# Layer 0 of a hybrid diffusion backbone: the linear recurrence's steps placed between the projections' units

## The chip, the cores and the metric

One core of one Trainium2 chip. The metric is device time in microseconds (us) of one execution of the whole program, the median of several runs. A profiled execution of the kernel before gives the spans, the busy times and the waits that are read here; "the profile" and "the trace" mean that execution.

## The reference, cut to what matters

Two layers over 512 sample tokens and 128 prompt tokens (640 in all), width 1024. The change touches layer 0 alone, the even one:

```python
def even_mixer(h, l, P, rope, ctx):
    z = jnp.dot(h, P['w_in_ab'][li])
    xa, ga, qd, kd, vd = split_last(z, (LRU_WIDTH, LRU_WIDTH, DIFF_QK, DIFF_QK, DIFF_V))   # 512 columns each
    y_a, lru_state = rglru_mixer(xa, ga, ...)
    q = rms_norm(qd), k = rms_norm(kd), v = vd       # per head; then rope on q and k of the sample
    o = diff_attention(q, k, v)
    y = concatenate([y_a, rms_norm(o) * (1 - lam_init)])
    return jnp.dot(y, P['w_out'][l])

def rglru_mixer(xa, ga, ...):
    u = centred_depthwise_conv(xa, conv_w) + conv_b             # 4 taps along the tokens
    # for each of two directions:
    r = sigmoid(u @ w_a + b_a);  i = sigmoid(u @ w_i + b_i)     # block-diagonal 64 x 64
    a = exp(-8 * r * softplus(-lam));  b = sqrt(1 - a**2) * (i * u)
    h = linear_recurrence(a, b, h0)                             # h[t] = a[t] h[t-1] + b[t]
    y = (h_f + h_b) * gelu(ga)
```

The modulation of both layers (shift, scale and gate, `silu(c) @ w_mod + b_mod`) does not depend on the tokens. The kernel computes it in 24 chunks of 512 columns, in the gaps that its order leaves.

## The kernel before, in words

All data is fp32. TensorE (PE), VectorE (DVE), ScalarE (ACT), GpSimd (POOL) and the DMA queue of SyncE (SP) each run an instruction order written out by hand; semaphores tie them together. Everything that PE produces goes to one of four PSUM pairs (two banks each), handed out in strict rotation (`take`, L168): the n-th unit of work gets pair n mod 4 and waits until the unit four places earlier was released by the engine that reads it (`release`, L183).

Layer 0's input projection is five chunks of 512 columns (2 MB of weights each). Chunks 0 (xa) and 1 (ga) are computed channel-major in four units each (`proj_T_pe`, L670: f = 0 to 3), chunks 2, 3, 4 (q, k, v) token-major in three units each (`proj_R_pe`, L689: two token tiles, two, one). ACT and DVE copy the units out in turns (`read_T` L712, `read_R` L722).

A modulation chunk i has four stages: PE multiplies (`mod_rows_pe`, L450), ACT copies the sums out (`mod_act`, L475), PE transposes them (`mod_turn_pe`, L466), DVE adds them up (`mod_dve`, L528). Chunks 4 to 7 stand between the five projections, chunks 8 to 13 inside the recurrence, chunks 14 to 19 inside the attention.

The recurrence (`lru_pe` L766, `lru_act` L783, `lru_dve` L823) comes after the last projection. It has eight steps i = 2 ct + d (four channel tiles, two directions). In a step PE computes two gate units (L773, L774), ACT does Tanh, Tanh, Exp, Tanh (L794 to L800) and later Sqrt (L805), and DVE does three elementwise operations (the "input", L831 to L834), then a multiply and two scans (L842 to L847) and, for d = 1, two adds and the product with gelu(ga) into `hT` (L853 to L857). Two sets of buffers (`lb`) alternate, so ACT's step i waits for DVE's scans of step i-2 (L793). ACT runs gates(i), then root(i-1); DVE runs input(i), then scan(i-1).

While the projections run, DVE does the convolution (L815) and, for q and then k, `diff_rows_dve` (L998): normalization over five tiles and rope, with ACT's Square and Sqrt in front (`diff_rows_act`, L939). After the recurrence `diff_pe` (L1065) transposes k and q, issues three filler matmuls (`keep_busy`, L1084) and starts the 20 steps of the attention with `scores` (L1089).

SP issues all weight loads in one order (`load_stream`, L1499). A chunk goes to one of three ring slots; before its load SP waits until PE has read the slot's previous chunk (`read_by_now`, L1495), and everything behind it in the order waits too. Before, slot = position mod 3:

```python
s = i % 3 if l == 0 or i < 6 else i % 2
```

Of the kernel before, what the change touches and what calls it, by code (L numbers as in the profile page):

```python
# [78 lines left out]
def build(nc, io, outs):  # L79
    with ExitStack() as ctx:  # L80
# [139 lines left out]
        def mmk(pe, out, lhs, rhs):  # L220

            for k in range(KD):
# [17 lines left out]
        for l in range(2):  # L240
            for i, c in enumerate(chunks[l]):
                s = i % 3 if l == 0 or i < 6 else i % 2
                slot_uses[s] += 1
                slot_of[c] = (s, slot_uses[s])
                loads.append((c, s, last_in_slot.get(s)))
                last_in_slot[s] = c
            base = list(slot_uses)
            for s in range(6):
                slot_uses[s] += NE // 2
                slot_of["exp", l, s] = base[s]  # L250
            loads.append((("experts", l), None, dict(last_in_slot)))
            for s in range(3):
                last_in_slot[s] = ("experts", l)
# [416 lines left out]
        def proj_T_pe(pe, l, c):  # L670

            w = arrived(pe, ("in", l, c, 0))
            for f in range(4):
                u = ("pT", l, c, f)
                ps = take(pe, u)
                lhs = lambda k: w[:, k, f * P:f * P + P]
                if l == 0 and c == 0 and f == 0:

                    for k in range(KD):
                        h_here(pe, l, 0, k)  # L680
                        pe.matmul(ps[:, 0:NS], lhs(k), hT[:, k, 0:NS], start=(k == 0), stop=(k == KD - 1))
                        last = pe.matmul(ps[:, NS:T], lhs(k), hT[:, k, NS:T], start=(k == 0), stop=(k == KD - 1))
                    finish(last, u)
                    continue
                mmk(pe, ps[:, 0:NS], lhs, lambda k: hT[:, k, 0:NS])
                finish(mmk(pe, ps[:, NS:T], lhs, lambda k: hT[:, k, NS:T]), u)
            chunk_last["in", l, c, 0] = u

        def proj_R_pe(pe, l, c):  # L689

            w = arrived(pe, ("in", l, c, 0))
            n = chunk_src(("in", l, c, 0))[1]
            for tp in range(3):
                u = ("pR", l, c, tp)
                ps = take(pe, u)
                if l == 1 and c == 4 and tp == 0:

                    keep_busy(pe, ps, 2)
                    for k in range(KD):
                        h_here(pe, l, 0, k)  # L700
                        for t in range(2):
                            last = pe.matmul(ps[:, 512 * t:512 * t + n], hT[:, k, t * P:t * P + P], w[:, k, 0:n],  # L702
                                             start=(k == 0), stop=(k == KD - 1))
                    finish(last, u)
                    continue
                for t in range(2 * tp, min(2 * tp + 2, NT)):
                    o = 512 * (t % 2)
                    last = mmk(pe, ps[:, o:o + n], lambda k: hT[:, k, t * P:t * P + P], lambda k: w[:, k, 0:n])
                finish(last, u)
            chunk_last["in", l, c, 0] = u  # L710

        def read_T(eng, l, c, dst, part, padded):  # L712
            for f in range(part, 4, 2):
                u = ("pT", l, c, f)
                ps = filled(eng, u)
                if padded:
                    copy(eng, dst[:, f, PS0:PS0 + NS], ps[:, 0:NS]).then_inc(S("pad_evac" + str(part)), 1)
                    release(copy(eng, dst[:, f, PP0:PP0 + NP], ps[:, NS:T]), u)
                else:
                    release(copy(eng, dst[:, f, :], ps[:, 0:T]), u)  # L720

        def read_R(eng, l, c, dst, part):  # L722
            n = chunk_src(("in", l, c, 0))[1]
            if l == 0 and c == 2:
                eng.wait_ge(S("y_room0"), 16)
                eng.wait_ge(S("y_room1"), 16)
            for tp in range(3):
                if (tp + c) % 2 == part:
                    u = ("pR", l, c, tp)
                    ps = filled(eng, u)  # L730
                    m = 2 if tp < 2 else 1
                    release(copy(eng, dst[:, 2 * tp:2 * tp + m, :],
                                 ps.rearrange("p (a b) -> p a b", a=2)[:, 0:m, 0:n]), u)
# [9 lines left out]
        lb = [[hflat[:, 2560 + 0 * UW:2560 + UW], hflat[:, 2560 + UW:2560 + 2 * UW],  # L743
               hflat[:, 2560 + 2 * UW:2560 + 3 * UW], ar(7716, UW)],
# [21 lines left out]
        def lru_pe(pe):  # L766
            pe.wait_ge(S("late_here"), LATE_ALL)
            for ct in range(4):
                pe.wait_ge(S("u_ready"), ct + 1)
                for q in range(4):  # L770
                    u = ("gate", ct, q)
                    ps = take(pe, u)
                    pe.matmul(ps[:, 0:NS], wg[:, q, ct, :], uT[:, ct, 0:NS], start=True, stop=True)  # L773
                    finish(pe.matmul(ps[:, NS:UW], wg[:, q, ct, :], uT[:, ct, NS:UW], start=True, stop=True), u)  # L774
                    if q % 2 == 1:

                        i = 2 * ct + q // 2
                        if i < N_LRU_MODS:
                            mod_rows_pe(pe, 8 + i)
                        if i <= N_LRU_MODS:  # L780
                            mod_turn_pe(pe, 7 + i)

        def lru_act(act, step):  # L783
            act.wait_ge(S("qk_rows"), 1)
            for i in range(9):
                if i < 8:
                    ct, d = i // 2, i % 2
                    tr, ti, a, _ = lb[i % 2]
                    c8 = 4 * d + ct
                    if i == 0:  # L790
                        filled(act, ("pR", 0, 4, 2))
                    if i >= 2:
                        act.wait_ge(S("lru_scan"), i - 1)  # L793
                    release(act.activation(tr, filled(act, ("gate", ct, 2 * d))[:, 0:UW], ACT.Tanh, scale=0.5,  # L794
                                           bias=hba[:, c8:c8 + 1]), ("gate", ct, 2 * d))
                    release(act.activation(ti, filled(act, ("gate", ct, 2 * d + 1))[:, 0:UW], ACT.Tanh, scale=0.5,
                                           bias=hbi[:, c8:c8 + 1]), ("gate", ct, 2 * d + 1))
                    emptied(act, ("gate", ct, 2 * d))
                    step(act.activation(a, tr, ACT.Exp, scale=hs[:, c8:c8 + 1], bias=hs[:, c8:c8 + 1]))
                    act.activation(tr, tr, ACT.Tanh, scale=hs[:, c8:c8 + 1], bias=hs[:, c8:c8 + 1])\  # L800
                        .then_inc(S("lru_tanh"), 1)
                if i >= 1:
                    act.wait_ge(S("lru_q"), i)
                    tr = lb[(i - 1) % 2][0]
                    act.activation(tr, tr, ACT.Sqrt, scale=-0.25).then_inc(S("lru_root"), 1)  # L805
                if i < N_LRU_MODS:
                    mod_act(act, 8 + i)
# [7 lines left out]
        def lru_conv_dve(v, step):  # L815
            for part in range(2):
                v.wait_ge(S("pad_evac" + str(part)), 2)
            for ct in range(4):
                emptied(v, ("pT", 0, 0, ct))
                conv_dve(v, step, uT[:, ct, :], xap[:, ct, :], lambda tap: cB[:, lw_col + 4 * tap + ct:lw_col + 4 * tap + ct + 1],  # L820
                         cB[:, cb_col + ct:cb_col + ct + 1]).then_inc(S("u_ready"), 1)

        def lru_dve(v, step):  # L823
            filled(v, ("pR", 0, 4, 2))
            v.wait_ge(S("u_ready"), 4)
            for i in range(9):
                if i < 8:

                    tr, ti, a, w = lb[i % 2]
                    v.wait_ge(S("lru_tanh"), i + 1)  # L830
                    step(v.tensor_tensor(w, a, a, ALU.mult))  # L831
                    v.scalar_tensor_tensor(out=tr, in0=w, scalar=1.0, in1=tr, op0=ALU.add, op1=ALU.mult)\
                        .then_inc(S("lru_q"), 1)
                    step(v.scalar_tensor_tensor(out=ti, in0=ti, scalar=1.0, in1=uT[:, i // 2, :], op0=ALU.add,  # L834
                                                op1=ALU.mult))
                if i >= 1:
                    j = i - 1
# [1977 lines left out]
```

## Time and profile before

| what | us |
|---|---|
| median of 3 runs | 1795.73 (1794.01 to 1798.09) |
| the profiled execution's own time | 1794.16 |
| its span, first to last instruction | 1791.7 |
| PE busy in the span | 1607.9 (90%) |
| DVE / ACT / POOL busy | 633.5 / 439.5 / 239.3 |
| mean granted TensorE clock | 0.953 |

A row of the windows view gives a stretch, its length, then busy us (and instructions) of PE, PE's weight loads, DVE, ACT and POOL, the granted TensorE clock (1.00 is 2.4 GHz, 0.50 is 1.2 GHz), the share of the DMA engines and GB/s. A timeline row gives start, duration, engine, line and operation, and in brackets the idle time before it and what ended it; neighbouring instructions overlap by some hundredths, so the text takes differences of starts where it can.

Times in the text are positions in the span of 1791.7 us. The 2.5 us between the span and the execution's time lie outside what the trace shows and are taken as unchanged; the median of the three runs stands 1.57 us above the profiled execution.

### The profile page before, as it was taken

The numbers are of one execution on the slowest core, as the hardware profiler recorded it, in microseconds if no ns is written. First come the engines' busy times: TensorE is split into PE (matmuls) and PEld (weight loads), VectorE is DVE, ScalarE is ACT, GpSimd is POOL, SyncE is SP. The second block draws the span as 40 slices with busy tenths as digits, with TensorE's granted clock in tenths as the row PEclk, the third lists the DMA queues.
The fourth block names the chain that finished last, engine by engine and source line by source line (L and its number), as shares of the span: only waits on it lengthen the run. The fifth ranks groups of instructions, "written<-read, shape, count | busy, mean of one in ns | idle before, by whom it ended". The sixth has DMA issues, their size and how long they took to land.

```text
span 1791.7 us, 37993 instructions
## 1 busy us (share of the span) xinstructions
PE 1607.9 (90%) x16758; PEld 1040.3 (58%) x16758; DVE 633.5 (35%) x1290; ACT 439.5 (25%) x734; POOL 239.3 (13%) x237
## 2 busy tenths in 40 slices
PE   5999976999959999999999989888899959999992
PEld 2554434664527677676555558666675536776761
DVE  4234466652260000003129646645462270000003
ACT  3211175551031111102110246432231031111110
POOL 0000000000001111100000026156440000111113
PEclk8999997999969999998999999999899979999996
DMA  9932281244218999994121100011115227999994
GB/s 341 307 115 94 100 288 46 95 142 188 94 74 307 385 382 394 380 379 143 47 71 71 50 1 1 1 50 50 49 50 200 73 85 247 372 388 387 386 394 142
DMA packets 90319, 330.09 MB, mean 184 GB/s; under 512 B 10708, under 2 KB 16456, under 8 KB 82024
## 3 DMA queue, kind: packets, MB, share of 16 engines
q1 hardware_dynamic: 76016, 287.29, 42.1%
q0 software_dynamic: 9168, 32.65, 6.6%
q10 hardware_dynamic: 5032, 8.65, 1.3%
q8 instruction: 80, 1.31, 0.3%
q14 instruction: 23, 0.19, 0.0%
HBM read 303.79 MB, written 24.78 MB: 183 GB/s over the span
## 4 chain that ended last, share of the span: by engine, by line
PE 83%; DVE 9%; ACT 3%; issue 2%; DMA 2%; POOL 0%; ACTq 0%; DVEq 0%
PE pairs L223 27%; PE pairs L1396 16%; PE pairs L1408 12%; PE pairs L1379 2%; PE pairs L343 2%; PE pairs L1096 2%; PE pairs L1110 1%; PE pairs L1886 1%; PE pairs L1866 1%; PE pairs L2093 1%; PE pairs L1849 1%; PE pairs L490 1%; PE pairs L461 1%; PE pairs L2104 1%; PE pairs L702 1%
## 5 line engine op out<-in xcount | busy, mean ns | idle before, releaser
L223 PE MATMUL pairs<-hT,ring 128*128 128x128 f32 (+1 forms) x1120 | 306.2, 436 | 2.2 <-ACT hT L357 2.2
L223 PEld LDWEIGHTS pairs<-hT,ring 128*128 128x128 f32 x1120 | 170.3, 192 | 139.0 <-issue 139.0
L357 ACT ACTIVATE arena<-pairs 128x512 f32<-128x512 f32 (+6 forms) x212 | 123.7, 602 | 430.3 <-PE pairs L223 198.8
L223 PE MATMUL pairs<-ring,hT 128*128 128x512 f32 (+1 forms) x448 | 177.4, 557 | 0.0
L1396 PEld LDWEIGHTS pairs<-arena,ring 128*64 128x64 f32 x4096 | 142.9, 137 | 13.6 <-issue 13.6
L1396 PEld LDWEIGHTS pairs<-arena 128*64 128x64 f32 x4096 | 142.8, 137 | 13.2 <-issue 13.1
L1396 PE MATMUL pairs<-arena 128*64 128x80 f32 x4096 | 145.5, 233 | 1.6 <-ACT arena L1431 1.0
L1396 PE MATMUL pairs<-arena,ring 128*64 128x80 f32 x4096 | 145.8, 233 | 0.5 <-issue 0.5
L223 PEld LDWEIGHTS pairs<-ring,hT 128*128 128x128 f32 x448 | 84.8, 190 | 92.1 <-issue 89.1
L1464 DVE TENSOR_SCALAR hT<-pairs,arena 80x512 f32<-80x512 f32 x32 | 23.9, 747 | 272.0 <-ACT hT L1440 272.0
L1408 PE MATMUL pairs<-ring,arena 128*80 128x512 f32 x256 | 112.7, 593 | 0.2 <-DMA ring<-in_exp_w 0.2
L1408 PE MATMUL pairs<-arena 128*80 128x512 f32 x256 | 112.5, 592 | 0.0
L1460 DVE TENSOR_TENSOR arena<-hT,pairs 128x160 f32<-128x160 f32 x64 | 20.5, 321 | 249.3 <-PE pairs L1396 249.3
L357 DVE COPY arena<-pairs 128x512 f32<-128x512 f32 (+7 forms) x37 | 25.2, 703 | 185.1 <-PE pairs L223 178.7
L1491 POOL DMA_INDIRECT moe_rows<-hT,arena x32 | 45.4, 1420 | 293.7 <-DVE hT L1464 293.7
L1408 PEld LDWEIGHTS pairs<-ring,arena 128*80 128x80 f32 x256 | 37.7, 152 | 63.1 <-issue 62.9
L1408 PEld LDWEIGHTS pairs<-arena 128*80 128x80 f32 x256 | 37.8, 153 | 62.6 <-issue 62.6
L1440 ACT ACTIVATE hT<-pairs,arena 80x512 f32<-80x512 f32 x32 | 21.9, 683 | 212.1 <-PE pairs L1408 212.1
L1431 ACT ACTIVATE arena<-pairs 128x640 f32<-128x640 f32 x32 | 22.5, 703 | 185.6 <-PE pairs L1379 185.6
L1189 DVE SCALAR_TENSOR_TENSOR xT<-pairs,modt,xT 128x512 f32<-128x512 f32 x24 | 18.0, 750 | 140.8 <-PE pairs L223 125.7
L343 PE MATMUL pairs<-cst 128*128 128x512 f32 x118 | 63.4, 680 | 3.8 <-ACT arena L357 2.1
L1481 POOL DMA_INDIRECT hT<-h_rows,arena x32 | 29.4, 917 | 241.3 <-PE pairs L1379 199.5
(393 smaller groups left out, 2139.6 us busy)
## 6 DMA issues: line engine op xcount, KB each, us to landing
arena<-in_exp_w SPq DMA_DIRECT2D x48, 2048.0 KB, 18.8
ring<-in_exp_w SPq DMA_DIRECT2D x48, 2048.0 KB, 20.1
ring<-in_w_mod SPq DMA_DIRECT2D x24, 2048.0 KB, 8.2
ring<-in_w_in_ab SPq DMA_DIRECT2D x5, 2048.0 KB, 11.9
ring<-in_w_in_cd SPq DMA_DIRECT2D x5, 2048.0 KB, 7.8
ring<-in_w_out SPq DMA_DIRECT2D x4, 2048.0 KB, 8.8
moe_rows<-arena POOLq DMA_DIRECT2D x2, 2560.0 KB, 12.8
h_rows<-arena POOLq DMA_DIRECT2D x2, 2560.0 KB, 8.2
```

Source lines behind the costliest of these rows:

```text
L223: last = pe.matmul(out, lhs(k), rhs(k), start=(k == 0), stop=(k == KD - 1))
L343: pe.matmul(ps[:, 0:512], ident, cst[:, 0:4, :].rearrange("p a b -> p (a b)"), start=True, stop=True)
L357: return eng.activation(dst, src, ACT.Copy) if eng is nc.scalar else eng.tensor_copy(dst, src)
L1096: pe.matmul(ps[:, 0:512], q, k[:, 0:512], start=True, stop=True)
L1379: last = pe.transpose(ps[:, o:o + CAP], xe[par][:, k::KD], ident[0:CAP, 0:CAP])
L1396: last = pe.matmul(lin_of(j, f)[c:c + 64, :], w[:, k, f * P + c:f * P + c + 64], rhs, start=(k == 0), stop=(k == KD - 1))
L1408: last = pe.matmul(PSUM[0:CAP, 3, 512 * half:512 * half + 512], hid[par][:, f, :], w2[:, f, 512 * half:512 * half + 512], start=(f == 0), ...
L1431: act.activation(xeT[par], ps, ACT.Copy).then_inc(pair_free[0], 1)
L1440: act.activation(ye[par][:, 0:512], PSUM[0:CAP, 3, 0:512], ACT.Copy, scale=gateT[:, bass.ds(i, 1)])\
L1464: v.tensor_scalar(ye[par][:, 512:1024], PSUM[0:CAP, 3, 512:1024], gateT[:, bass.ds(i, 1)], None, ALU.mult).then_inc(pair_free[3], 1)
L1481: g.indirect_dma_start(xe[e % 2], None, DR["h", l], off(e)).then_inc(S(f"gathered{e % 2}"), 16)
L1491: g.indirect_dma_start(DR["m", l], off(e), ye[e % 2], None, compute_op=ALU.add)\
```

## The change

1. The order of loads and their slots are given by a list. From modulation chunk 4 to chunk 13, ten chunks, all go through slot 2, one after the other; the projections' chunks alternate between slots 1 and 0.
2. The projections are cut into single units (`proj_T_one`, `proj_R_one`, `read_T_one`, `read_R_one`), and the recurrence into `gates_pe`, `lru_gates_act`, `lru_root_act`, `lru_conv_dve(ct)`, `lru_input_dve(i)`, `lru_scan_dve(j)`. Three new functions, `layer0_pe`, `layer0_act` and `layer0_dve`, write out one order each, with a pair of gate units behind projection units from (1, 0) to (3, 0) and modulation chunks 4 to 13 between them.
3. `diff_rows` of q and of k come after the recurrence on ACT and DVE. The product with gelu(ga) is done for all four channel tiles after the last scan, into a tile `yT` of its own; ACT copies it to `hT` in steps 4 to 7 of the attention, and the output projection waits for these copies.
4. `lb`'s first set and rope's scratch move to other places of the arena; the sum of the two directions goes back into `uT`.

The diff, cut to its core:

```diff
-        N_LRU_MODS = 6
-        chunks = [all_mods[:4] + [c for p in zip(ins[0], all_mods[4:8]) for c in p] + ins[0][4:] + all_mods[8:20] +
-                  wouts[0], ins[1] + all_mods[20:] + wouts[1]]
+        chunks = [all_mods[:4] + ins[0][0:1] + all_mods[4:5] + ins[0][1:2] + all_mods[5:6] + ins[0][2:3] +
+                  all_mods[6:8] + ins[0][3:4] + all_mods[8:11] + ins[0][4:5] + all_mods[11:20] + wouts[0],
+                  ins[1] + all_mods[20:] + wouts[1]]
+        first_slots = [0, 1, 2, 0, 1, 2, 0, 2, 1, 2, 2, 0, 2, 2, 2, 1, 2, 2, 2, 0, 2, 1, 0, 2, 1, 0, 2]
...
-                s = i % 3 if l == 0 or i < 6 else i % 2
+                s = first_slots[i] if l == 0 else i % 3 if i < 6 else i % 2
...
+        yT = ar(9480, 4, T)
+        lb = [[ar(i * UW, UW) for i in range(4)],
...
+        def gates_pe(pe, i):
+            ct = i // 2
+            if i == 0:
+                pe.wait_ge(S("late_here"), LATE_ALL)
+            pe.wait_ge(S("u_ready"), ct + 1)
+            for q in (2 * (i % 2), 2 * (i % 2) + 1):
+                u = ("gate", ct, q)
+                ps = take(pe, u)
+                pe.matmul(ps[:, 0:NS], wg[:, q, ct, :], uT[:, ct, 0:NS], start=True, stop=True)
+                finish(pe.matmul(ps[:, NS:UW], wg[:, q, ct, :], uT[:, ct, NS:UW], start=True, stop=True), u)
...
+        def layer0_pe(pe):
+            for f in range(4):
+                proj_T_one(pe, 0, 0, f)
+            mod_rows_pe(pe, 4)
+            proj_T_one(pe, 0, 1, 0)
+            mod_turn_pe(pe, 4)
+            gates_pe(pe, 0)
+            proj_T_one(pe, 0, 1, 1)
+            mod_rows_pe(pe, 5)
+            gates_pe(pe, 1)
+            proj_T_one(pe, 0, 1, 2)
+            mod_turn_pe(pe, 5)
+            gates_pe(pe, 2)
+            proj_T_one(pe, 0, 1, 3)
+            mod_rows_pe(pe, 6)
+            gates_pe(pe, 3)
+            for tp in range(3):
+                proj_R_one(pe, 0, 2, tp)
+                mod_turn_pe(pe, 6 + tp)
+                mod_rows_pe(pe, 7 + tp)
+                gates_pe(pe, 4 + tp)
+            proj_R_one(pe, 0, 3, 0)
+            mod_turn_pe(pe, 9)
+            mod_rows_pe(pe, 10)
+            gates_pe(pe, 7)
+            proj_R_one(pe, 0, 3, 1)
+            mod_turn_pe(pe, 10)
+            proj_R_one(pe, 0, 3, 2)
+            mod_rows_pe(pe, 11)
+            for tp in range(2):
+                proj_R_one(pe, 0, 4, tp)
+                mod_turn_pe(pe, 11 + tp)
+                mod_rows_pe(pe, 12 + tp)
+            proj_R_one(pe, 0, 4, 2)
+            mod_turn_pe(pe, 13)
...
+        def layer0_act(act, step):
...
+            mod_act(act, 9)
+            lru_gates_act(act, step, 6)
+            lru_root_act(act, 5)
+            mod_act(act, 10)
+            lru_gates_act(act, step, 7)
+            lru_root_act(act, 6)
+            lru_root_act(act, 7)
+            act.wait_ge(S("y_first"), 4)
+            diff_rows_act(act, 0)
+            read_R_one(act, 0, 3, qkv_of(3), 1)
+            mod_act(act, 11)
+            diff_rows_act(act, 1)
+            read_R_one(act, 0, 4, qkv_of(4), 0)
+            mod_act(act, 12)
+            mod_act(act, 13)
+            read_R_one(act, 0, 4, qkv_of(4), 2)
...
+        def layer0_dve(v, step):
+            read_T_one(v, 0, 0, xap, 1, True)
+            lru_conv_dve(v, step, 0)
+            lru_conv_dve(v, step, 1)
+            read_T_one(v, 0, 0, xap, 3, True)
+            lru_conv_dve(v, step, 2)
+            lru_conv_dve(v, step, 3)
+            mod_dve(v, step, 4)
+            lru_input_dve(v, step, 0)
+            read_T_one(v, 0, 1, ga, 1, False)
+            lru_input_dve(v, step, 1)
+            lru_scan_dve(v, step, 0)
...
+            read_R_one(v, 0, 3, qkv_of(3), 0)
+            mod_dve(v, step, 9)
+            lru_input_dve(v, step, 7)
+            lru_scan_dve(v, step, 6)
+            lru_scan_dve(v, step, 7)
+            v.wait_ge(S("gelu"), 1)
             for ct in range(4):
...
+                v.tensor_tensor(yT[:, ct, :], uT[:, ct, 0:T], ga[:, ct, :], ALU.mult).then_inc(S("y_first"), 1)
+            v.wait_ge(S("y_first"), 4)
+            diff_rows_dve(v, step, 0)
+            mod_dve(v, step, 10)
+            read_R_one(v, 0, 3, qkv_of(3), 2)
+            diff_rows_dve(v, step, 1)
+            mod_dve(v, step, 11)
+            read_R_one(v, 0, 4, qkv_of(4), 1)
+            mod_dve(v, step, 12)
+            mod_dve(v, step, 13)
...
+                if 4 <= i < 8:
+                    act.activation(hT[:, i - 4, :], yT[:, i - 4, :], ACT.Copy).then_inc(S("y_here"), 1)
...
-                pe.wait_ge(S("y_first"), 4)
+                pe.wait_ge(S("y_here"), 4)
```

## Rows read from the trace of the kernel before

**Rows 1.** Windows: projections, recurrence, hand-over, attention; each engine's busy us, granted clock, DMA.

```profile
79.40:226.40 147.00, 147.00 (x445) 67.99 (x445) 58.44 (x105) 17.30 (x17) 0.58 (x1) 1.00 0.33 117
226.40:296.50 70.10, 43.03 (x211) 21.33 (x209) 50.34 (x83) 52.91 (x61) 0.56 (x1) 0.84 0.60 214
296.50:304.80 8.30, 7.40 (x29) 5.69 (x29) 3.21 (x4) 3.14 (x4) 0.90 (x1) 0.67 0.06 1
320.00:400.00 80.00, 79.03 (x463) 49.88 (x461) 49.23 (x120) 39.47 (x92) 0.00 (x0) 1.00 0.38 132
```

**Rows 2.** Chain in order of time, one recurrence step: start, us, engine, line.

```profile
258.04 0.80 ACT hT L794
...
261.32 0.84 DVE arena L831
...
265.97 0.44 DVE arena L847
266.43 0.80 ACT arena L794
```

**Rows 3.** PE's timeline: from the recurrence's end to the first scores.

```profile
297.40 0.48 PE L1074 MATMUL pairs<-cst,dk_c 128*128 128x128 f32 x1 [8.47 <-ACT arena L357]
...
304.78 1.12 PE L1096 MATMUL pairs<-arena 64*128 64x512 f32 x2
```

**Rows 4.** PE's timeline: a projection of each kind, a turn, a product, a gate pair.

```profile
81.26 34.88 PE L223 MATMUL pairs<-hT,ring 128*128 128x512 f32 x128
115.98 0.60 PE L472 MATMUL pairs<-cst,arena 128*128 128x128 f32 x4
116.51 1.92 PE L461 MATMUL pairs<-ring,csil 128*32 128x512 f32 x16
118.36 34.60 PE L223 MATMUL pairs<-ring,hT 128*128 128x512 f32 x80
...
226.44 1.02 PE L773 MATMUL pairs<-arena 128*128 128x512 f32 x2
...
228.70 1.92 PE L461 MATMUL pairs<-ring,csil 128*32 128x512 f32 x16
```

**Rows 5.** ACT's timeline, inside the recurrence, with its table loads.

```profile
244.46 1.28 ACT L805 ACT_TABLE_LOAD   x1
245.75 0.74 ACT L805 ACTIVATE arena<-arena 128x643 f32<-128x643 f32 x1
```

**Rows 6.** DVE's timeline: inputs, scans and sums of one step of the second direction.

```profile
244.47 0.83 DVE L831 TENSOR_TENSOR arena<-hT 128x643 f32<-128x643 f32 x1 [2.71 <-ACT hT L800]
...
246.94 0.83 DVE L842 TENSOR_TENSOR arena<-arena 128x643 f32<-128x643 f32 x1
...
249.76 0.69 DVE L853 TENSOR_TENSOR hT<-arena 128x512 f32<-128x512 f32 x1
...
250.81 0.82 DVE L857 TENSOR_TENSOR hT<-hT,arena 128x640 f32<-128x640 f32 x1
```

**Rows 7.** ACT's timeline: Square in front of k's rows.

```profile
192.70 2.33 ACT L902 ACTIVATE arena<-arena 128x2560 f32<-128x2560 f32 x1
```

**Rows 8.** DVE's timeline: rows of k, from the square sums to rope's end.

```profile
195.15 2.82 DVE L908 TENSOR_REDUCE sm<-arena 128x40 f32<-128x2560 f32 x1 [4.34 <-ACT arena L902]
...
215.04 0.06 DVE L354 MEMSET sm<- 128x1 f32 x1
```

**Rows 9.** Windows of 3 us around a spell of idle PE before the output projection.

```profile
410.00:413.00 3.00, 1.57 (x8) 0.94 (x7) 1.25 (x2) 1.10 (x2) 0.00 (x0) 0.71 0.00 0
413.00:416.00 3.00, 2.55 (x3) 1.17 (x4) 0.00 (x0) 0.09 (x1) 0.00 (x0) 0.50 0.82 257
416.00:419.00 3.00, 3.00 (x6) 1.35 (x5) 0.00 (x0) 0.00 (x0) 0.00 (x0) 0.65 1.03 437
```

**Rows 10.** Loads by L1513: issue to landing in two stretches, 60 to 160 and 188 to 300.

```profile
DMA to landing us min/median/max: 7.9/10.9/12.8
...
DMA to landing us min/median/max: 8.0/8.9/10.8
```

More of the change, by code:

```diff
@@ L670, in proj_T_pe @@
         def proj_T_pe(pe, l, c):
-            w = arrived(pe, ("in", l, c, 0))
             for f in range(4):
[L674 to L686, printed above, removed]
@@ L687, in proj_T_pe, with proj_T_one @@
-            chunk_last["in", l, c, 0] = u
+                proj_T_one(pe, l, c, f)
+        def proj_T_one(pe, l, c, f):
+            w = arrived(pe, ("in", l, c, 0)) if f == 0 else chunk(("in", l, c, 0))
+            u = ("pT", l, c, f)
+            ps = take(pe, u)
+            lhs = lambda k: w[:, k, f * P:f * P + P]
+            chunk_last["in", l, c, 0] = u
+            if l == 0 and c == 0 and f == 0:
+                for k in range(KD):
+                    h_here(pe, l, 0, k)
+                    pe.matmul(ps[:, 0:NS], lhs(k), hT[:, k, 0:NS], start=(k == 0), stop=(k == KD - 1))
+                    last = pe.matmul(ps[:, NS:T], lhs(k), hT[:, k, NS:T], start=(k == 0), stop=(k == KD - 1))
+                finish(last, u)
+                return
+            mmk(pe, ps[:, 0:NS], lhs, lambda k: hT[:, k, 0:NS])
+            finish(mmk(pe, ps[:, NS:T], lhs, lambda k: hT[:, k, NS:T]), u)
@@ L689, in proj_R_pe, with proj_R_one @@
         def proj_R_pe(pe, l, c):
-            w = arrived(pe, ("in", l, c, 0))
+            for tp in range(3):
+                proj_R_one(pe, l, c, tp)
+        def proj_R_one(pe, l, c, tp):
+            w = arrived(pe, ("in", l, c, 0)) if tp == 0 else chunk(("in", l, c, 0))
             n = chunk_src(("in", l, c, 0))[1]
[L693 to L708, printed above, removed]
-                finish(last, u)
@@ L710, in proj_R_pe @@
-            chunk_last["in", l, c, 0] = u
+            u = ("pR", l, c, tp)
+            ps = take(pe, u)
+            chunk_last["in", l, c, 0] = u
+            if l == 1 and c == 4 and tp == 0:
+                keep_busy(pe, ps, 2)
+                for k in range(KD):
+                    h_here(pe, l, 0, k)
+                    for t in range(2):
+                        last = pe.matmul(ps[:, 512 * t:512 * t + n], hT[:, k, t * P:t * P + P], w[:, k, 0:n],
+                                         start=(k == 0), stop=(k == KD - 1))
+                finish(last, u)
+                return
@@ L712, in read_T @@
+            for t in range(2 * tp, min(2 * tp + 2, NT)):
+                o = 512 * (t % 2)
+                last = mmk(pe, ps[:, o:o + n], lambda k: hT[:, k, t * P:t * P + P], lambda k: w[:, k, 0:n])
+            finish(last, u)
         def read_T(eng, l, c, dst, part, padded):
             for f in range(part, 4, 2):
[L714 to L720, printed above, removed]
+                read_T_one(eng, l, c, dst, f, padded)
@@ L764, in conv_dve @@
             return ins
-        def lru_pe(pe):
-            pe.wait_ge(S("late_here"), LATE_ALL)
-            for ct in range(4):
[L769 to L807, printed above, removed]
@@ new lines, in lru_gates_act @@
+        def lru_gates_act(act, step, i):
+            ct, d = i // 2, i % 2
+            tr, ti, a, _ = lb[i % 2]
+            c8 = 4 * d + ct
+            if i == 0:
+                act.wait_ge(S("u_ready"), 4)
+            if i >= 2:
+                act.wait_ge(S("lru_scan"), i - 1)
+            release(act.activation(tr, filled(act, ("gate", ct, 2 * d))[:, 0:UW], ACT.Tanh, scale=0.5,
+                                   bias=hba[:, c8:c8 + 1]), ("gate", ct, 2 * d))
+            release(act.activation(ti, filled(act, ("gate", ct, 2 * d + 1))[:, 0:UW], ACT.Tanh, scale=0.5,
+                                   bias=hbi[:, c8:c8 + 1]), ("gate", ct, 2 * d + 1))
+            emptied(act, ("gate", ct, 2 * d))
+            step(act.activation(a, tr, ACT.Exp, scale=hs[:, c8:c8 + 1], bias=hs[:, c8:c8 + 1]))
+            act.activation(tr, tr, ACT.Tanh, scale=hs[:, c8:c8 + 1], bias=hs[:, c8:c8 + 1])\
+                .then_inc(S("lru_tanh"), 1)
@@ new lines, in lru_root_act @@
+        def lru_root_act(act, i):
+            act.wait_ge(S("lru_q"), i + 1)
+            tr = lb[i % 2][0]
+            act.activation(tr, tr, ACT.Sqrt, scale=-0.25).then_inc(S("lru_root"), 1)
+        def layer0_pe(pe):
[14 more added lines that the diff above has]
+            gates_pe(pe, 3)
+            for tp in range(3):
+                proj_R_one(pe, 0, 2, tp)
[16 more added lines that the diff above has]
+            mod_turn_pe(pe, 13)
@@ new lines, in qkv_of @@
+        def qkv_of(c):
+            return qkv[:, :, 512 * (c - 2):512 * (c - 1)]
+        def layer0_act(act, step):
+            read_T_one(act, 0, 0, xap, 0, True)
+            read_T_one(act, 0, 0, xap, 2, True)
+            mod_act(act, 4)
+            read_T_one(act, 0, 1, ga, 0, False)
+            lru_gates_act(act, step, 0)
+            mod_act(act, 5)
+            lru_gates_act(act, step, 1)
+            lru_root_act(act, 0)
+            read_T_one(act, 0, 1, ga, 2, False)
+            lru_gates_act(act, step, 2)
+            lru_root_act(act, 1)
+            mod_act(act, 6)
+            lru_gates_act(act, step, 3)
+            lru_root_act(act, 2)
+            act.wait_ge(S("y_room0"), 16)
+            act.wait_ge(S("y_room1"), 16)
+            read_R_one(act, 0, 2, qkv_of(2), 0)
+            mod_act(act, 7)
+            lru_gates_act(act, step, 4)
+            lru_root_act(act, 3)
+            gelu_act(act)
+            mod_act(act, 8)
+            lru_gates_act(act, step, 5)
+            lru_root_act(act, 4)
+            read_R_one(act, 0, 2, qkv_of(2), 2)
+            mod_act(act, 9)
[14 more added lines that the diff above has]
+            read_R_one(act, 0, 4, qkv_of(4), 2)
@@ L813, in gelu_act @@
             act.activation(ga, ga, ACT.Gelu_apprx_tanh).then_inc(S("gelu"), 1)
[L815 to L821, printed above, removed]
@@ L1005, in diff_rows_dve @@
             mark(v).then_inc(S(("dq_done", "cache_k_ready")[j]), 1)
-            rope_dve(v, step, x[:, 0:ST], 8, ar(7716, 2048))
+            rope_dve(v, step, x[:, 0:ST], 8, ar(2584, 2048))
             if j:
@@ L2618, in _ @@
                     mod_turn_pe(pe, 3)
[L2619 to L2624 removed]
                 if l == 0:
[L2626 removed]
+                    layer0_pe(pe)
                     diff_pe(pe)
                 else:
+                    for _, _, c, _ in ins[1]:
+                        (proj_T_pe if c < 3 else proj_R_pe)(pe, 1, c)
                     decay_pe(pe)
```

144 lines of the change are left out of this document (67 added, 77 removed).

## The prediction

> **What bounds the kernel now.** I read the windows view first. From 79.4 to 226.4 PE is busy all the time at full clock, while DVE is busy 58.4 us of 147 and ACT 17.3. In the recurrence, 226.4 to 296.5, it is the other way round: PE 43.0 of 70.1 at a mean clock of 0.84, DVE 50.3, ACT 52.9 [rows 1]. So two neighbouring stages have opposite limits. The chain of waits says what sets the second one: Tanh to Tanh on ACT (258.04 to 261.32, 3.28 us), then DVE's input and scan (to 266.41), then ACT's next gates at 266.43: 8.39 us a step, eight steps, on the path [rows 2]. It is a latency loop; neither engine fills it. The attention behind is PE's again (79.0 of 80 us) [rows 1]; its first scores start at 304.78 [rows 3]. All that follows hangs on that start, so the sum is about when the scores begin.
>
> **PE's own work.** The projections from 79.4 keep their length, 147 us. Added between them, at prices of a full clock: eight gate pairs at 2.26 us (226.44 to 228.70) = 18.1; the products of six chunks (8 to 13, `mod_rows_pe`) at 1.85 (116.51 to 118.36) = 11.1; seven turns (7 to 13) at 0.53 (115.98 to 116.51) = 3.7 [rows 4]. Sum 32.9: without waits the projections end at 226.5 + 32.9 = 259.4.
>
> **Does the recurrence keep up?** A T unit costs 34.88/4 = 8.7, an R unit of two tiles 34.6 x 2/5 = 13.8, of one tile 6.9 [rows 4]. Adding in the new order from 79.4, gates 0 end at 92.8 and gates 7 at 196.8. The distances between pairs are 11.5 (T unit and a turn) to 18.4 us (R unit, turn and product), with 11.5 once more before gates 6. The loop needs 8.39 [rows 2] plus one or two copies and a modulation read, each under 0.9 us by the operations of like size [rows 5, 6]: about 10.5. It fits every distance, with 1 us to spare in the tightest. The PSUM rotation lets PE run four units ahead, and each unit's reader falls to the same distances, so I cost PE's waits up to gates 7 at nothing; if that cover is gone they are rival 3.
>
> **DVE's tail.** The normalization and rope of q and k (`diff_rows`) were hidden under projections (DVE idle 88 of 147 us) [rows 1]; now they come after the last scan, and PE waits for what is queued behind them on DVE. From 196.8: ACT's last activations 2.6 (3.28 less the first, 0.7); DVE input 2.5 (244.47 to 246.94); scan 6 2.8 (246.94 to 249.76) and scan 7 with its sums 3.9 (to 250.81) [rows 6]; four products of 640 columns at 0.75 to 0.82, 3.0; Square 2.3 [rows 7]; then reduction to rope's end 19.9 (195.15 to 215.04) [rows 8]. That is 233.8 for q. Reading modulation 10 and unit (3, 2) is about 1.1. For k: 2.3 + 19.9, done at 257.1, modulation 11 at 257.5.
>
> PE meanwhile: from 196.8 unit (3, 1), turn 10, (3, 2), product 11, (4, 0) reach 233.7. Turn 11 needs the pair of turn 10, released by DVE at 234.2: 0.5 lost. Product 12 needs the pair of (3, 2): 0.1. Unit (4, 1) and turn 12 run to 251.0. Product 13 needs the pair of turn 11, which DVE reads only after k's normalization and rope, at 257.5: **6.5 us of idle PE**. Sum of waits 7.1: the projections end at 266.5. ACT's reads in between come earlier, since ACT's part of `diff_rows` ends with the Sqrt.
>
> **Clock.** A spell in which PE was busy 1.57 of 3 us was followed by 0.50 in the next 3 us and 0.65 in 3 more [rows 9], some 5 us of work at 1.2 GHz, 2.5 us lost. The idle 6.5 us are longer; bounds are 0 and 9.3 (product 13, (4, 2) and turn 13 wholly at half). I take 3, near the row: 269.5. The steps before gain clock instead (0.84 to 1.00), which is in the prices already.
>
> **Hand-over.** Before, half of the transposes of k and q ran before the recurrence's end; now all 44 come at the end: 44 x 0.133 = 5.9 (a turn is four in 0.53), three fillers of two 512-column passes each at 34.6/80 = 0.43, 2.6 [rows 4], and two reads before and after, 0.8 each: 10.1 in all. Scores start at 279.6, against 304.78: **25.2 us gained**.
>
> **What moves at no price.** SP: a load of a w_mod chunk waits for the read of the one before, and the projection chunks queue behind these. Distances between reads are 14 us or more except from chunk 8 to 9 (gates 2.3, unit (2, 2) 6.9, turn 0.5 = 9.7); landing takes 8.0 to 10.8 us, 8.9 in the middle [rows 10]: it just fits. Chunks 3 and 4 of the projection are issued right behind chunks 7 and 10 and have 16 us or more. Chunks 14 to 19 and w_out keep their places inside the attention. POOL: its two cache outputs and the state's go out some 40 us later or 80 us earlier, and their next reader is the norm behind the output projection, over 100 us on. ACT: four copies of y, 0.74 each by an activation of 643 columns [rows 5], one per attention step, where ACT is busy 39.5 of 80 us [rows 1]; all exposed they would cost 3.0, below nothing they cannot go. Rope's other scratch and the other buffers: nothing, the operations are the same.
>
> **A rule against the row.** ACT goes between Tanh and Sqrt in each step, and a load starts 1.29 us before the Sqrt that follows it [rows 5]. The Trainium skill (ScalarE: Activation LUTs, What ACT_TABLE_LOAD costs) budgets about 2.66 us for each switch, 1.38 of it a drain. The sum uses the row. By the page the Sqrt of step 6 would come some 0.8 us after DVE is ready for it and the sum would give 24.4; no drain shows in this trace.
>
> **Total.** 1794.16 - 25.2 = 1769.0 on the profiled execution's scale; the median stands 1.57 above it, so 1770.5.
>
> **Rivals.**
> 1. The tail does not show: DVE gets ahead or the clock holds, and PE is the bound to the end. For it: DVE is the only late engine and 7 us are few against 60. Against: the order puts both reads behind k's `diff_rows`. 7.1 + 3 less: 1760.4.
> 2. The one slot is late. Landing at the 12.8 us of two loads issued together [rows 10] makes chunk 9 late by 3.5, and PE's idle may cost clock as above, 3: 1777. For it: one distance fits by a hair. Against: chunk 9 loads alone.
> 3. **Slower.** PE, handed its pairs strictly in turn, waits at each recurrence step as it does in the stage of before: 70.1 - 43.0 = 27.1 us idle, and 43.0 us busy for 32.9 us of added work and 2.9 of 22 early transposes, so 7.2 lost to the clock [rows 1]. If both come back between 90 and 197, the scores start at 279.6 + 34.3, 9.1 later than before: 1794.2 + 9.1 + 1.6 = 1805. It decides at 25 us of such waits, 3 a step. For it: 1 us of slack in the T part. Against: 7.9 us in the R part. The Trainium skill (TensorE: Matmul & The Clock Gate, A second HAM failure mode: psum-queue depth-cycling) holds that short idles while PSUM is cycled let the clock swing between its levels; the recurrence's 0.84 agrees, the projections' 1.00, on the same rotation, do not.
> 4. The change does not do what it says: a wait carried over holds the attention where it was, or it loses the time in its steps. 1795. Nothing in the rows speaks for it.
>
> **Chances.** A measurement of this kernel tells 0.2%, 3.6 us, from no change. Forecast 0.66, rival 1 0.12, rival 2 0.10, rival 3 0.08, rival 4 0.04. Faster 0.88, same 0.04, slower 0.08. The range takes in rivals 1 and 2 and the bounds of clock (-3, +6) and copies (+3), with the loop's slack of 1 us a step lost once: 1758 to 1786.
>
> **What would show it.** In the trace of after: PE without idle and at 1.00 from 79 to about 234; gates 7 ending near 197; one wait of some 6 us on DVE before the product of chunk 13; a granted clock near 0.5 for a few us behind it; first scores near 280; attention, experts and layer 1 of the same lengths. Waits of over 1 us before each gate pair, or a wait of PE on the ring's DMA, would make the prediction wrong.

## The result, and the profile after

| | before | after |
|---|---|---|
| median, runs of one comparison, us | 1796.72 of 4 (1794.01 to 1798.09) | 1766.78 of 4 (1765.78 to 1770.26) |
| the profiled execution's own time | 1794.16 | 1770.26 |
| its span | 1791.7 | 1768.3 |
| PE busy in the span | 1607.9 (90%) | 1600.7 (91%) |
| DVE / ACT / POOL busy | 633.5 / 439.5 / 239.3 | 634.2 / 441.0 / 238.9 |
| mean granted TensorE clock | 0.953 | 0.957 |

The ratio after to before is 0.9839, interval 0.982 to 0.9857: faster by 1.6%. A second measurement (`after_again` below) gave 0.9847, 0.9827 to 0.9867. The forecast was 1770.5 us, with a range of 1758 to 1786; over the median shown then, 1795.73, it is a ratio of 0.986.

DVE, ACT and POOL are busy nearly as long as before. PE is busy 7.2 us less with the same 16758 instructions, at a higher mean clock; the other 16 of the 23.4 us are PE's idle time that went. As in the prediction, a product and a turn are PE's multiplication and transposition of one modulation chunk, unit (c, n) is unit n of the projection's chunk c, and gates i is the pair of gate units of recurrence step i. The windows of the kernel after, with the columns of [rows 1], cut at the end of the last gate pair, the end of the projections and the first scores:

```profile
81.80:198.70 116.90, 116.90 (x441) 55.94 (x441) 49.41 (x78) 53.16 (x59) 0.00 (x0) 1.00 0.47 164
198.70:272.40 73.70, 65.07 (x194) 27.40 (x192) 52.39 (x100) 15.32 (x18) 0.58 (x1) 0.95 0.40 144
272.40:280.40 8.00, 7.60 (x52) 5.85 (x51) 3.65 (x6) 3.51 (x5) 1.45 (x2) 1.00 0.95 291
```

PE is busy in all of the first 116.9 us, at full clock, with the gates of all eight recurrence steps among its work; DVE's last sum of the recurrence ends at 211.7. The 73.7 us behind hold 8.6 us of idle PE, the hand-over 0.4. PE's waits from the product of chunk 4 to the first scores, all of them (who waits and for whom, us in total, times, longest):

```profile
PE pairs L462 <- DVE modt L541: 6.7, 1, 6.7
PE pairs L473 <- DVE modt L541: 1.9, 1, 1.9
PE pairs L1192 <- issue: 0.4, 1, 0.4
```

PE's timeline: the product of chunk 4, and the tail, which answers to [rows 3, 4]:

```profile
81.82 1.92 PE L462 MATMUL pairs<-ring,csil 128*32 128x512 f32 x16
...
198.50 0.39 PE L782 MATMUL pairs<-arena 128*128 128x131 f32 x2
...
237.65 0.63 PE L473 MATMUL pairs<-cst,arena 128*128 128x128 f32 x4 [1.94 <-DVE modt L541]
...
261.23 3.64 PE L462 MATMUL pairs<-ring,csil 128*32 128x512 f32 x16 [6.69 <-DVE modt L541]
264.80 7.23 PE L223 MATMUL pairs<-ring,hT 128*128 128x512 f32 x16
271.86 0.60 PE L473 MATMUL pairs<-cst,arena 128*128 128x128 f32 x4
272.87 0.30 PE L1192 MATMUL pairs<-cst,dk_c 128*128 128x128 f32 x1 [0.40 <-issue]
...
277.70 2.74 PE L344 MATMUL pairs<-cst 128*128 128x512 f32 x6
280.37 1.12 PE L1214 MATMUL pairs<-arena 64*128 64x512 f32 x2
```

Both waits end with L541, DVE's sum of a modulation chunk (`mod_dve`). DVE's timeline shows where these sums stand: the first behind q's rope, the second behind k's. Reduction (L1024) to the end of rope is 20 us, the sum 0.17.

```profile
211.72 3.03 DVE L927 TENSOR_TENSOR arena<-arena 128x640 f32<-128x640 f32 x4
217.25 2.82 DVE L1024 TENSOR_REDUCE sm<-arena 128x40 f32<-128x2560 f32 x1 [2.50 <-ACT arena L1018]
...
237.33 0.17 DVE L541 TENSOR_TENSOR modt<-sm,cA 128x8 f32<-128x8 f32 x1
...
240.74 2.82 DVE L1024 TENSOR_REDUCE sm<-arena 128x40 f32<-128x2560 f32 x1 [2.64 <-ACT arena L1018]
...
260.92 0.17 DVE L541 TENSOR_TENSOR modt<-sm,cA 128x8 f32<-128x8 f32 x1
```

**Where the time came from.** I measure one stage in every kernel: from the start of the product of chunk 4 to the first scores. Before, it is 79.41 to 304.78, 225.4 us; after, 81.82 to 280.37, 198.55 us: 26.8 gained, and 198.4 in the second measurement. Its start before:

```profile
79.41 1.92 PE L461 MATMUL pairs<-ring,csil 128*32 128x512 f32 x16
```

The attention behind keeps its length (scores to output projection 108.7 before, 108.25 after). The span is shorter by 23.4 only: the profiled execution of after came to the stage 2.4 us later (the last section says why), and from the output projection to the end it took 1379.7 us for 1378.3. That last part took 1372.6 to 1380.2 us in the nine profiled executions of the changed kernel and its versions, so a whole time can differ by some us from what the stage says. The stage is read from one execution of each kernel.

### The profile page after: what moved, and what is told of

Its sections match the earlier page's. It is cut to its first block, busy times and chain, and to the rows that moved or that the text cites. A ratio compares the mean times of both kernels' runs of the same rounds, so it can differ in the third digit from the quotient of the medians.

```text
span 1768.3 us, 38026 instructions
## 1 busy us (share of the span) xinstructions
PE 1600.7 (91%) x16758; PEld 1036.6 (59%) x16758; DVE 634.2 (36%) x1290; ACT 441.0 (25%) x736; POOL 238.9 (14%) x237
## 4 chain that ended last, share of the span: by engine, by line
PE 71%; DVE 8%; DMA 3%; issue 2%; ACT 2%; POOL 0%; ACTq 0%; DVEq 0%; SPq 0%
PE pairs L223 18%; PE pairs L1514 15%; PE pairs L1526 12%; PE pairs L1497 2%; PE pairs L1214 2%; DMA ring<-in_exp_w 2%; PE pairs L1228 1%; PE pairs L2004 1%; PE pairs L1984 1%; PE pairs L2211 1%; PE pairs L344 1%; PE pairs L1967 1%; PE pairs L491 1%; PE pairs L2222 1%; PE pairs L706 1%
## 5 line engine op out<-in xcount | busy, mean ns | idle before, releaser
L1526 PEld LDWEIGHTS pairs<-ring,arena 128*80 128x80 f32 x256 | 37.6, 152 | 63.4 <-issue 63.1
L358 DVE COPY arena<-pairs 128x512 f32<-128x512 f32 (+7 forms) x37 | 25.2, 703 | 125.6 <-PE pairs L223 120.7
L344 PE MATMUL pairs<-cst 128*128 128x512 f32 x118 | 59.6, 645 | 3.7 <-ACT arena L358 2.1
L622 ACT ACTIVATE arena<-xT 128x640 f32<-128x640 f32 x32 | 23.3, 736 | 155.0 <-DVE xT L1310 135.7
```

Of the source, the lines that this page charges most:

```text
L344: pe.matmul(ps[:, 0:512], ident, cst[:, 0:4, :].rearrange("p a b -> p (a b)"), start=True, stop=True)
L358: return eng.activation(dst, src, ACT.Copy) if eng is nc.scalar else eng.tensor_copy(dst, src)
L622: act.activation(sq_all[:, k, :] if (l, n) == (1, 0) else sq[:, k % 2, :], xT[:, k, :], ACT.Square).then_inc(S("sq"), 1)
L1526: last = pe.matmul(PSUM[0:CAP, 3, 512 * half:512 * half + 512], hid[par][:, f, :], w2[:, f, 512 * half:512 * half + 512], start=(f == 0), ...
```

## The experiments

The theory: PE bounds the stage, the recurrence hides beside the projections with some slack, and what is left are two waits on modulation sums behind q's and k's rows.

**1 and 2. More DVE work in the steps, after and before.** Three more 512-column scans, of the same values, in steps 0 to 5: 18 scans of 1.3 us, some 23.5 us of DVE work.

```diff
+            for _ in range(3 if j < 6 else 0):
+                step(v.tensor_tensor_scan(h[:, 0:NS][:, r], a[:, 0:NS][:, r], ti[:, 0:NS][:, r],
+                                          cB[:, st_col + c8:st_col + c8 + 1], ALU.mult, ALU.add))
             v.tensor_tensor_scan(h[:, UP0:UW][:, r], a[:, UP0:UW][:, r], ti[:, UP0:UW][:, r], 0.0,
```

> The changed kernel with three more scans of 512 columns on DVE behind the scan of each of the steps 0 to 5 (they write the same values again): 6 x 3 x 1.3 = 23.5 us more work on DVE between 113 and 190. Theory (the loop is hidden under the projections, with room between DVE's steps of 4 to 7 us idle): PE shows no wait before gates 7, scores start where they did, 1766.8 +-2 us. Rival (PE waits for the loop through the PSUM rotation, the loop fits by 1 us a step): some 3 us a step, 1766.8 + 17 = 1784, with PE's waits on DVE or ACT between 93 and 199.

> The kernel before with the same three scans more in the steps 0 to 5. Theory (there the loop gates, input, scans is on the path, 8.39 us a step): all of it shows, each step grows by 3.9 us, 1796.7 + 23.5 = 1820. Rival (the stage was bound by PE's low clock or by the loads of w_mod, the loop only beside it): less than half of it, under 1808.

In the kernel before, 1816.84 us, ratio 1.0132 (1.0106 to 1.0157), the stage 249.8: 24.5 longer, so all of it shows. Tanh to Tanh is 12.4 us now, with the added scans (L848 there) in the chain of waits:

```profile
259.17 0.80 ACT arena L794
262.52 0.84 DVE arena L831
265.85 1.29 DVE arena L845
267.17 1.29 DVE arena L848
271.13 0.44 DVE arena L850
271.59 0.80 ACT hT L794
```

In the kernel after, 1777.77, ratio 0.9921 (0.99 to 0.9942), the stage 206.2: 7.7 longer, so in the stage two thirds were hidden. The medians of the whole time stand 11.0 us apart (1777.77 and 1766.78), and by the ratios it is 13 to 15, so what of this lies outside the stage is not shown. PE's waits there are the two tail ones as before, and two new ones in the steps:

```profile
PE pairs L462 <- DVE modt L541: 6.7, 1, 6.7
PE pairs L223 <- DVE modt L541: 2.3, 1, 2.3
PE pairs L223 <- DVE arena L358: 2.1, 1, 2.1
PE pairs L473 <- DVE modt L541: 2.0, 1, 2.0
```

The two new ones are 4.4 us; of the rest, low clock behind the second takes 1.7 (the unit there 15.58 instead of 13.89) and behind the last 1.1 (unit (4, 2) 8.30 instead of 7.23). So the same scans are on the path in one order and mostly off it in the other, but neither the full cover nor none was right: the slack per step is limited. DVE's timeline of after, at the inputs of steps 0, 1, 2, 3 and 6, shows it:

```profile
97.83 0.83 DVE L953 TENSOR_TENSOR arena<-arena 128x643 f32<-128x643 f32 x1 [4.37 <-ACT arena L798]
110.69 0.83 DVE L953 TENSOR_TENSOR arena<-arena 128x643 f32<-128x643 f32 x1 [5.92 <-ACT arena L798]
122.89 0.83 DVE L953 TENSOR_TENSOR arena<-arena 128x643 f32<-128x643 f32 x1 [5.26 <-ACT arena L798]
135.77 0.83 DVE L953 TENSOR_TENSOR arena<-arena 128x643 f32<-128x643 f32 x1 [5.70 <-ACT arena L798]
...
184.07 0.83 DVE L953 TENSOR_TENSOR arena<-arena 128x643 f32<-128x643 f32 x1 [5.06 <-ACT arena L798]
```

DVE is idle 4.4 to 7.3 us ahead of each of the eight inputs. Where the loop runs at its own pace, in the kernel before, such idle time is 2.7 us in the steps of one direction [rows 6] and 0.8 to 0.9 in those of the other:

```profile
252.93 0.83 DVE L831 TENSOR_TENSOR arena<-arena 128x643 f32<-128x643 f32 x1 [0.78 <-ACT arena L800]
```

The difference, some 2 to 6 us, is my estimate of the slack of a step. With the scans added, the idle time ahead of the inputs of steps 2 and 6 fell to that 2.70, ahead of step 3 to 1.59, and PE's new waits come right behind gates 3 and 6. The input of step 6 there:

```profile
185.41 0.83 DVE L953 TENSOR_TENSOR arena<-arena 128x643 f32<-128x643 f32 x1 [2.70 <-ACT arena L798]
```

**3. The same scans in steps 6 and 7 alone** (`j >= 6`): 7.8 us ahead of q's rows.

> The changed kernel with three more scans behind the scans of steps 6 and 7 alone, 7.8 us. Theory (from gates 7 on DVE's tail sets when PE gets the pairs of turns 10 and 11): all 7.8 us show, 1766.8 + 7.8 = 1774.6, as longer PE waits before turn 11 (1.9 to some 9.7) and the same one before product 13. Rival (PE's work is the bound to the end and the two waits are small change): under 3 us more.

1776.02, ratio 0.9915 (0.9894 to 0.9936), the stage 205.9: 7.4 longer. The delay shows nearly whole, but the wait stands elsewhere than expected. PE's waits:

```profile
PE pairs L223 <- ACT arena L358: 7.5, 1, 7.5
PE pairs L462 <- DVE modt L541: 6.7, 1, 6.7
```

The first is in front of unit (4, 0), whose pair is that of unit (3, 1). ACT reads (3, 1), but only behind its own part of q's rows, which waits for DVE's last product of y. So behind gates 7 PE hangs on DVE by two threads: through ACT's queue and through modulation 10. Unit (4, 0) then runs partly at low clock (16.41 us for 14.00), and the wait at turn 11 is gone, as PE came to it later: 7.5 + 2.4 - 1.9 = 8.0; product 13 and unit (4, 2) took 0.5 less than in the change, which leaves the 7.4. Product 13's 6.7 did not change: PE reached turn 11 at 245.51, just as DVE's sum of chunk 10 ended (245.37), so from there on both stand to each other as in the change.

**4. Is it the clock?** Three filler products (six matmul records) in front of each gate pair of the kernel before keep PE busy in its recurrence.

```diff
                     ps = take(pe, u)
+                    if q % 2 == 0:
+                        keep_busy(pe, ps, 3)
```

> The kernel before with three filler products of 512 columns on PE ahead of the first gate unit of each recurrence step (2.6 us a step at full clock), to hold the granted clock at 1.00 in the recurrence. Theory (ACT's and DVE's loop is the path there, not PE): the step stays at 8.4 us, scores start where they did or, if the transposes of k and q then run at full clock, up to 2 us earlier: 1794 to 1797. Rival (a good part of the gain was the clock, 0.84 to 1.00): 5 to 8 us faster, 1789 to 1792.

1801.24, ratio 1.0032 (1.0012 to 1.0052): no faster. The window that answers to the second of [rows 1]:

```profile
226.40:296.50 70.10, 59.51 (x263) 29.07 (x261) 43.94 (x73) 53.15 (x61) 0.56 (x1) 0.97 0.62 214
```

The granted clock is 0.97 for 0.84 and PE busy 59.5 us for 43.0, yet the later steps start every 8.4 us as before (ACT at 256.33, 264.80, 273.19, 281.59). The stage is 5.2 us longer, twice the 2.6 us of fillers ahead of a pair: those of the first two steps stand in front of the loop. The low clock within the recurrence cost nothing there, so its return is not where the change gains. The 22 late transposes behind the loop ran at the low clock in this run too (0.52 granted), so it does not test them: they took 4.7 us before (297.40 to 302.11) and all 44 take 4.8 after, from which I estimate some 2 us of the 26.8 for their clock.

**5 and 6. Taking the two waits away.** The short sum of a modulation chunk goes ahead of the long rows on DVE. First for chunk 11 alone (`after_mod11`):

```diff
             read_R_one(v, 0, 3, qkv_of(3), 2)
-            diff_rows_dve(v, step, 1)
             mod_dve(v, step, 11)
+            diff_rows_dve(v, step, 1)
```

> The changed kernel with one line moved: DVE sums modulation chunk 11 before it normalizes k, not after. Theory (DVE's order is what holds PE before product 13): the wait of 6.7 us and the low clock behind it (product 13 took 3.6 instead of 1.85) are gone, from product 4's start to the first scores 198.6 - 8.5 = 190.1 us, time 1766.8 - 8.5 = 1758. Rival (the next late thing, the read of unit (4, 1) behind k's rope or the rope itself, takes over): the wait moves to turn 13 or to the transposes of k, under 3 us gained.

Then also for chunk 10, whose neighbour, the read of unit (3, 2), goes to ACT (`after_tail`):

```diff
-            diff_rows_dve(v, step, 0)
             mod_dve(v, step, 10)
-            read_R_one(v, 0, 3, qkv_of(3), 2)
+            diff_rows_dve(v, step, 0)
...
             read_R_one(act, 0, 3, qkv_of(3), 1)
+            read_R_one(act, 0, 3, qkv_of(3), 2)
```

> The changed kernel with chunks 10 and 11 summed on DVE before q's and before k's normalization, and unit (3, 2) read by ACT instead of DVE. Theory: both of PE's waits (1.9 and 6.7) and the low clock (2.0) go, PE is busy without a gap from 79 to the last projection unit, 198.6 - 10.6 = 188.0 us from product 4's start to the first scores, time 1756. Rival (some of it comes back as a wait for ACT, which now has a read more in front of k's Square, or for the rope of k): 192 us or more, over 1760.

`after_mod11`: 1758.61, ratio 0.9794 (0.9774 to 0.9814), the stage 189.98, with the 1.94 us before turn 11 as its one wait left. `after_tail`: 1760.64, ratio 0.9799 (0.9777 to 0.9821), the stage 187.81. Both stages are as the theory had them; the whole time of `after_tail` is not (1756 was expected), and its five runs lie between 1752.11 and 1763.32. Up to the 0.4 us of issue ahead of the transposes PE does not wait at all in `after_tail`; its window from the product of chunk 4 to the end of the projections, and its timeline from turn 11 on:

```profile
81.50:261.30 179.80, 179.80 (x633) 82.97 (x632) 101.21 (x177) 68.97 (x77) 0.58 (x1) 1.00 0.47 165
```

```profile
235.20 0.60 PE L473 MATMUL pairs<-cst,arena 128*128 128x128 f32 x4
...
251.95 1.92 PE L462 MATMUL pairs<-ring,csil 128*32 128x512 f32 x16
253.80 7.13 PE L223 MATMUL pairs<-ring,hT 128*128 128x512 f32 x16
...
269.28 1.12 PE L1214 MATMUL pairs<-arena 64*128 64x512 f32 x2
```

So the two waits and the clock behind them cost 198.4 - 187.8 = 10.6 us of the stage. The place of one short sum in DVE's queue made 8.4 of them; the other 2.2 went with the second sum and the read of unit (3, 2), moved together.

**7. Is the one ring slot close to late?** The product of chunk 8 goes behind unit (2, 2), so its slot comes free some 9 us later and chunk 9's load is issued later by as much (`mod_act(8)` moves along).

```diff
                 proj_R_one(pe, 0, 2, tp)
+                if tp == 2:
+                    mod_rows_pe(pe, 8)
                 mod_turn_pe(pe, 6 + tp)
-                mod_rows_pe(pe, 7 + tp)
+                if tp != 1:
+                    mod_rows_pe(pe, 7 + tp)
```

> The changed kernel with the product of chunk 8 behind unit (2, 2) instead of in front of the gates before it (its sum on ACT moves behind it too), so that chunk 9's load has some 1.2 us instead of 9.7 between the read of chunk 8 and its own product. Theory (the loads through the one slot are hidden just by that distance, a load takes 8 to 9 us): PE waits some 7 us for the ring before product 9 and runs some us at the low clock behind it, 9 to 10 us more, 1776. Rival (the slot has room, a chunk is loaded well ahead): no wait on the ring, 1767 +-2.

1782.1, ratio 0.9916 (0.9891 to 0.994), the stage 209.25: 10.7 longer. PE's timeline at the product of chunk 9:

```profile
185.18 3.64 PE L462 MATMUL pairs<-ring,csil 128*32 128x512 f32 x16 [7.27 <-DMA ring<-in_w_mod]
```

The load was issued at 176.5 and landed 8.6 us later; the wait, 0.8 more at turn 8 and half a clock behind it (3.64 for 1.92) make 9.8 of the 10.7, and gates 6, partly at the low clock too, 1.0 more. The whole time is 13 us over the change's in the same comparison (1768.99), for the 9 to 10 expected. In the change itself chunk 9 is issued at 166.7, lands in 8.0 and is wanted at 176.2: 1.5 us to spare. The landings of all its loads, in the window 100 to 260, which answers to [rows 10]:

```profile
DMA to landing us min/median/max: 7.8/8.1/13.4
```

**8 to 10. Repeats.** The change again, and both better versions in another comparison.

> The changed kernel once more, beside the others on one chip: 198.6 us from product 4's start to the first scores, 0.984 of the kernel before, by every theory.

> The version with DVE's two sums moved forward and unit (3, 2) read by ACT, once more. Its stage was 187.8 us from product 4 to the first scores, 2.2 us less than with chunk 11's sum alone moved; if only that stage differs, 1756 +-2 us and 0.978 of the kernel before; if something behind it gives the 2.2 us back, the same time as the other version, 1758 to 1760.

> The version with chunk 11's sum alone moved, once more beside it: 190.0 us from product 4 to the first scores, 1758 +-2 us, 0.979 of the kernel before.

`after_again`: 1768.99, ratio 0.9847 (0.9827 to 0.9867), the stage 198.4, the same two waits. `after_tail_2`: 1758.97, 0.9789 (0.9773 to 0.9805), the stage 187.8. `after_mod11_2`: 1760.1, 0.9799 (0.9784 to 0.9813), the stage 191.6 and not 190.0: the same wait before turn 11 (1.95) was followed by the low clock there (0.58 granted from 239 to 242, product 12 in 3.2 us), while in `after_mod11` a wait of 1.94 was not (1.00, 1.86). What decides it is not shown. Both versions beat the change and the kernel before. In the stage `after_tail` is ahead by 2.2 us in one pair and 3.8 in the other; their whole times don't tell them apart, and 1758.97 is what was expected if something behind the stage gives the 2.2 us back. Nothing here shows such a thing: in both profiled executions of this version the part behind the attention is the shortest of all (1372.7 and 1372.6).

## Why the prediction was right

**PE's own work: right.** 147 + 32.9 = 179.9 us of projections and recurrence products were forecast; `after_tail`, which has no waits, measures 179.8 in its window.

**The recurrence keeps up: right.** PE never waited before turn 11. The margin forecast, 1 us in the tightest step, was small beside the one estimated from the trace (2 to 6 us, 2.4 in the tightest): of 23.5 us of added scans PE's waits show 4.4. What hid the recurrence is shown by experiments 1 and 2 together: the same work in the loop costs 24.5 us before and 7.7 after.

**DVE's tail: right in kind and nearly in size.** Product 13 waited 6.69 (6.5 forecast), at the place and for the reason given. Turn 11 waited 1.94 instead of 0.5, as small errors on both sides added up: PE came to it 0.4 us earlier than forecast and DVE's sum of chunk 10 some 1 us later. Product 12 did not wait (0.1).

**Clock: mis-sized.** I took 3 us from a stretch nearby; it was 1.8: product 13 took 3.57 from start to start for 1.85 in `after_tail`, unit (4, 2) 7.06 for 6.97. The windows behind the wait answer to [rows 9]:

```profile
255.00:258.00 3.00, 0.00 (x0) 0.00 (x0) 2.90 (x9) 0.00 (x0) 0.00 (x0) 1.00 0.00 0
258.00:261.00 3.00, 0.00 (x0) 0.00 (x0) 2.83 (x10) 0.00 (x0) 0.00 (x0) 0.53 0.00 0
261.00:264.00 3.00, 2.77 (x16) 0.68 (x16) 1.48 (x4) 0.00 (x0) 0.00 (x0) 0.50 0.01 3
264.00:267.00 3.00, 3.00 (x12) 1.15 (x6) 0.00 (x0) 0.60 (x1) 0.00 (x0) 0.83 0.28 53
```

Part of the low spell fell into the idle time itself, where it costs nothing, and the clock was back some 0.2 us into unit (4, 2) (granted 0.50 from 264.5 to 265.0, 0.98 from there to 265.5).

**Hand-over: mis-sized, the largest error.** 7.9 us for 10.1. The 44 transposes took 4.8 (272.87 to 277.70), 0.11 each and not the 0.133 of a turn of four, and PE did not stand still for the two reads of 0.8: 0.4 us of issue in front, and scores right behind the fillers.

**The sum.** Waits +1.5, clock -1.2, hand-over -2.2: a stage 1.9 us shorter than forecast by these terms, 1.6 by its length (26.8 gained for 25.2). Against `after_tail`, 187.8 + 8.6 of waits + 1.8 of clock = 198.2, of 198.55 measured.

The stage is so well hit in part by luck, since the three mis-sized terms partly cancel. The median is further off, 3.7 us under the forecast, and the stage's 1.6 are the lesser part of that. The profiled execution of after took 1770.26 for 1769.0: a later start of the stage and a longer rest took back more than the 1.6. And the forecast set the median 1.57 us above the profiled execution, as it stood before; after, the profiled execution is the slowest of the four, 3.5 us above the median.

**No price: right where measured.** The attention is not longer (108.25 us for 108.7), so ACT's copies of y cost nothing. Chunk 9's load came 1.5 us ahead of its use, close to the 0.8 of a distance of 9.7 and a landing of 8.9.

**The rule against the row.** The load ahead of the Sqrt of step 6 starts at 202.44 and its Sqrt at 203.74, on ACT's timeline:

```profile
202.44 1.28 ACT L804 ACT_TABLE_LOAD   x1
203.74 1.37 ACT L804 ACTIVATE arena<-arena 128x643 f32<-128x643 f32 x2
```

That is 1.30 a switch, as in [rows 5], with ACT busy until the load. The Trainium skill (ScalarE: Activation LUTs, What ACT_TABLE_LOAD costs) has 2.66; the measurement decides. The 0.8 us by which the sum would have been less did not come either: DVE goes from the input of step 7 to scan 6 without a wait (L956 ends at 204.95, L964 starts at 204.99).

**The rivals.** Rival 1 is what `after_tail` makes true: 1760.4 was its price, 1760.64 and 1758.97 were measured (its stage gained 37.6 us where the price has 35.3); in the change as it is, it fell. Rival 2 names a real danger, 1.5 us away, that did not decide; experiment 7 shows that where the load is late, PE pays for it and for the clock. Rival 3 fell at once: PE, on the same rotation of pairs, had no idle time and a granted clock of 1.00 from 81.8 to 235.7. The Trainium skill (TensorE: Matmul & The Clock Gate, A second HAM failure mode: psum-queue depth-cycling) describes short idles that swing the clock; this trace has no such idles beside the recurrence, so it does not show it. Rival 4 fell with the result: the stage is 26.8 us shorter.

## What to carry to other kernels

A latency loop that leaves its engines partly idle (DVE busy 50.3 and ACT 52.9 of 70.1 us here) cost PE no wait beside a stage that PE bounds, where the distance between its steps, 11.4 us and more, exceeded its own period; count that distance step by step, and what else its engines read in it. Where pairs are handed out in strict turn, a release of 0.4 us of work queued behind 20 us of other work stopped the producer for 6.7 us: put short releases ahead of long work that nobody waits for yet. Here that was worth another 0.5% on top of the change.

## What was not expected of the hardware

The first projection unit of layer 0 starts behind 3.3 us of idle PE in every kernel, and its first pair of 512-column matmul records takes 1.10 us in some executions and 2.05 in others, with the same program text up to there. PE's timelines of before and of after:

```profile
44.63 1.10 PE L681 MATMUL pairs<-hT,ring 128*128 128x512 f32 x2 [3.33 <-ACT hT L632]
```

```profile
44.18 2.05 PE L684 MATMUL pairs<-hT,ring 128*128 128x512 f32 x2 [3.34 <-ACT hT L633]
```

The granted clock from 44 to 50 is 0.50 in after (1.2 GHz) and 1.00 in before (2.4 GHz). In after the unit's first three k steps take 6.2 us, in before 3.3, so the low level costs 2.9 there. `before_scan0to5` shows 2.04 and `after_scan0to5` 1.10, and `before_fill` begins with 1.10 and has 1.65 and 1.91 right behind it, so it belongs to the execution and not to the change. It is why after reaches the product of chunk 4 at 81.82 and before at 79.41, and most of why the spans differ by less than the stages. What decides it was not tried; nor was what else scatters the runs of one kernel over 4 to 12 us, which hides the 2.2 us between the two better versions.
